# Depthwise-convolution products moved to ScalarE, branch projections reordered, attention block interleaved and finished by token rows

## The chip, the cores and the metric

The kernel runs on one core of a Trainium2 chip. The metric is the device time of one execution in microseconds (us). All weights and inputs come from HBM, and everything is float32.

## The reference, cut to what matters

Two transformer-like blocks follow each other on a 512 x 1024 activation. Each sublayer ends in a residual and a norm. The parts that the change touches are the middle sublayer of the first block and the last sublayer of the second:

```
u = modulate(x, sh2, sc2)
xr, gr, conf_in, gate_a, gate_b = split(u @ w_in)
xr = causal_depthwise_conv(xr, rnn_conv_w, rnn_conv_b)      # 4 taps
hr = rg_lru(xr, ...)                                        # gates r, i, then a scan over time
ya = (hr * gelu(gr)) @ rnn_w_proj
glu = conf_in[..., :D] * sigmoid(conf_in[..., D:])
hb = causal_depthwise_conv(glu, conf_dw_w, conf_dw_b)       # 31 taps
yb = silu(layer_norm(hb)) @ conf_w_proj
merged = sigmoid(gate_a) * ya + sigmoid(gate_b) * yb
x = layer_norm(alpha * x + (1 + g2) * (merged @ mix_w_out))
...
x = x + concat(ret, ssm) @ w_out
q = rms_norm(x, norm2_g) @ wq                               # 4 heads of 256
p = softmax(q k^T / 16);  o = p v                           # memory of 256 rows
x = x + o @ wo
return rms_norm(x, norm_f_g)
```

## The kernel before

Activations lie feature-major: eight tiles `[128 features, 512 tokens]` each. Every product `u @ W` is done in fp32r with both operands split into a high and a low part, `hi*hi + lo*hi + hi*lo`. So a chunk of 256 output features is 2 tiles x 8 k-tiles x 3 = 48 matmuls of 128x512. A weight chunk is loaded by SP into one of two raw slots, split high by ScalarE (`hi_step`, L559) and low by VectorE (`lo_step`, L978). `hi_step(ph, i, m, j)` prepares the chunk that stands two behind the one of that name, because it waits until TensorE has finished with the slot (`mm`). The order on each engine is written out by hand; engines meet at semaphores only. A PSUM bank pair is handed back through `free0`/`free1`.

The middle sublayer. TensorE's order is conf (8 chunks), xr (4), gr (4), the 16 r/i gate matmuls, gb (4), ga (4), the mean matmul `ln_shift(1)` (L1851), ya (4), the norm's statistics, yb (4), mix (4). The 31-tap convolution is done tile by tile beside them:

- GpSimd has tiles 0 to 2 (`POOL_CONV = 3`). Each tap is a `tensor_scalar` product into `conv_tap` (L464) and a `tensor_tensor` sum into `conv_out` (L466), each waiting for the one before it.
- VectorE has tiles 3 to 7. Each tap is one `scalar_tensor_tensor` whose accumulator is a PSUM bank (L1244), placed in batches (`conv_taps(n)`) between its other steps. Others of its steps are the 4-tap convolution (L1270, L1273: both tensor operands in SBUF), the products of the gated scan (L1302 to L1307) and the weight splits.
- GpSimd then sums the tiles for the mean (L430), which TensorE waits for before its first ya chunk.
- The sigmoid gates of gb and ga go to DRAM (`gate`, L721) and wait there for `bt_step` 16, because their staging tile lies over `rnn_i`. They come back as `sig_gate_a` and `sig_gate_b`.

The attention sublayer. After the eight residual tiles of wout_s, the root of the mean square is computed, then the eight tiles are scaled and split (L1407, L811, L1417), and only then does wq start. After wq the four heads run one behind the other: scores (L2143), row maximum (L1722), exponentials (L950), scaling (L1731), transposes (L2159), a copy (L955), values (L2166), a copy to `xa_out` (L1737) and its split. Then wo (4 chunks), the last norm's sums (L1877), the root, eight scaled tiles (L1749, L965), 32 transposes (L2177), and four stores of 512 KB.

Of the kernel before, what the change touches and what calls it, by code (L numbers as in the profile page):

```python
# [26 lines left out]
P = 128  # L27
D = 1024
KT = D // P
L = 512  # L30
# [8 lines left out]
POOL_CONV = 3  # L39
# [20 lines left out]
PHASES = [("ffn1", 22, 11), ("down1", 16, 4), ("conf", 8, 4), ("xr", 4, 2), ("gr", 4, 2),  # L60
          ("gb", 4, 2), ("ga", 4, 2), ("ya", 4, 2), ("yb", 4, 2), ("mix", 4, 2),
# [35 lines left out]
def build_program(nc, I, out):  # L97
    ctx = ExitStack()
    with ctx:
        BASE = 16512  # L100

        def at(name, kb, shape, dt=F32):
# [20 lines left out]
        TAP = at("conv_tap", H0 + 85, [P, L])  # L123
# [5 lines left out]
        STG = at("stage4k", H0 + 81, [P, 2, L])  # L129
# [9 lines left out]
        G = at("gelu_gate", T0, [P, KT, L])  # L139
        SGA = at("sig_gate_a", T0, [P, KT, L])  # L140
        SGB = at("sig_gate_b", T0, [P, KT, L])
# [98 lines left out]
        PS = ctx.enter_context(nc.psum_tensor("ps", [P, 8, 512], F32))  # L240
        MODP = PS[:, 4, 0:ADA_ALL]
# [18 lines left out]
                 "yb_sum mg_hi mg_lo lam_step conv31 conv31p s5_load s5_pow_load s5_expand s5_t "  # L260
# [5 lines left out]
                 "s_sum p_scaled p_t pt_ready o_mm oa_ready oh ol yo_ready out_t or_ready out_store "  # L266
# [15 lines left out]
        def _(sp):  # L282
# [82 lines left out]
            simple("gr", I["w_in"], D)  # L365
            simple("gb", I["w_in"], 5 * D)
            simple("ga", I["w_in"], 4 * D)
            simple("ya", I["rnn_w_proj"])
# [20 lines left out]
            for t in range(TT):  # L389
                sp.wait_ge(s["or_ready"], t + 1)  # L390
                sp.dma_start(out[0, t * P:(t + 1) * P, :], OR[:, t]).then_inc(s["out_store"], 16)
            sp.wait_ge(s["out_store"], 16 * TT)
# [3 lines left out]
        def _(pool):  # L396
# [55 lines left out]
            for f in range(POOL_CONV):  # L452
                pool.wait_ge(s["free1"], UB["conf"] + f // 2 + 1)
                if f == 0:
                    pool.wait_ge(s["pads_ready"], 1)
                for k in range(CONV_C):
                    src = GLU[:, f, k + 2:k + 2 + L]
                    w = col("conf_dw_w_a", 8 * k + f)
                    n = (2 * CONV_C - 1) * f + 2 * k
                    if k == 0:  # L460
                        nc.gpsimd.tensor_scalar(HB[:, f], src, w, col("conf_dw_b", f), ALU.mult, ALU.add).then_inc(s["conv31p"], 1)
                        continue
                    pool.wait_ge(s["conv31p"], n - 1)
# [5 lines left out]
            ln_sum(1, HB, lambda f: (s["conv31p"], (2 * CONV_C - 1) * (f + 1)) if f < POOL_CONV else  # L469
                   (s["conv31"], CONV_C * (f + 1 - POOL_CONV)))  # L470
# [74 lines left out]
            pool.dma_start(SGS[:], sgs_dram).then_inc(s["sgs_load"], 16)  # L545
            pool.wait_ge(s["mm"], CB["wq"])
            pool.dma_start(KA[:], ka_dram).then_inc(s["kv_load"], 16)
# [4 lines left out]
        def _(act):  # L552
# [21 lines left out]
            def ln_root(c):  # L574

                A(EPSC[:, 4 + c:5 + c], EPSC[:, 1:2], ACT.Sqrt)
                act.wait_ge(s["m_done"], c + 1)
                xsum = ln_tiles(c)[0]
                A(xsum[:], PS[:, 5], ACT.Square).then_inc(s["msq"], 1)
                act.wait_ge(s["var_ready"], c + 1)  # L580
                A(RT[:], xsum[:], ACT.Sqrt, bias=EPSC[:, 0:1]).then_inc(s["root_ready"], 1)
# [98 lines left out]
            with act.Fori(0, 4) as i:  # L680
# [6 lines left out]
            act.wait_ge(s["pads_ready"], 2)  # L687
            with act.Fori(0, 2) as i:
                for j in range(2):
                    hi_step("xr", i, 2, j)  # L690
                    act.wait_ge(s["mm"], CB["xr"] + 2 * i + j + 1)
                    A(XR[:, bass.ds(4 * i + 2 * j, 2), 8:8 + L], PS[:, 2 * j:2 * j + 2], ACT.Copy).then_inc(free[j], 1)
            with act.Fori(0, 2) as i:
                for j in range(2):
                    hi_step("gr", i, 2, j)
                    act.wait_ge(s["mm"], CB["gr"] + 2 * i + j + 1)
                    A(G[:, bass.ds(4 * i + 2 * j, 2)], PS[:, 2 * j:2 * j + 2], ACT.Gelu_apprx_tanh).then_inc(free[j], 1)

            for f in range(KT):
# [25 lines left out]
            gate("gb", sgb_dram, 0, 1)
# [15 lines left out]
            hi_step("ya", 0, 2, 1)
            hi_step("ya", 1, 2, 0)
            ln_squares(1, HB, 0, 7)
            hi_step("ya", 1, 2, 1)
            ln_squares(1, HB, 7, 8)
            ln_root(1)
            for f in range(KT + 1):
                if f < KT:
                    act.wait_ge(s["xn_ready"], 8 + f + 1)
                    A(HB[:, f], HB[:, f], ACT.Silu, scale=col("conf_ln_g", f), bias=col("conf_ln_b", f)).then_inc(s["conf_silu"], 1)  # L750
                if f:
                    act.wait_ge(s["conf_silu"], f)
# [187 lines left out]
            split_only("wout_s", 2, 2)  # L940
            norm(5, lambda f: pair_tile("wout_s", f), X, 1)

            rms_hi(4, 40, "norm2_g_2")
            plain("wq", QA)
            for h in range(XH):
                act.wait_ge(s["smax_ready"], 2 * h + 2)
                if h:
                    act.wait_ge(s["p_t"], h)
                for t in range(TT):
                    A(PB[:, t], PS[:, 4 + t // 2, (t % 2) * MEM:(t % 2 + 1) * MEM], ACT.Exp, scale=1.0 / 16, bias=XS[:, 1, t:t + 1],  # L950
                      accum_out=XS[:, 2 + h % 2, t:t + 1]).then_inc(s["exp_done"], 1)
                act.wait_ge(s["p_t"], h + 1)
# [3 lines left out]
                act.wait_ge(s["oa_ready"], h + 1)  # L956
                A(UH[:, 2 * h:2 * h + 2], OA[:], ACT.Copy).then_inc(s["oh"], 1)
            for i in range(2):
                for j in range(2):
                    if i == 0:  # L960
                        hi_step("wo", 0, 2, j)
            norm(6, lambda f: pair_tile("wo", f), X, 1)
            for f in range(KT):
                act.wait_ge(s["xn_ready"], 48 + f + 1)
# [1249 lines left out]
```

## Time and profile before

| | us |
|---|---|
| median of three runs (2372.64 to 2377.97) | 2374.69 |
| the profiled execution | 2371.09 |
| its span in the trace | 2369.1 |
| PE busy | 1953.8 (82%) |
| DVE busy | 1205.8 (51%) |
| ACT busy | 743.1 (31%) |
| POOL busy | 488.9 (21%) |

The span is what lies between the first and the last instruction; 2.0 us lie around it. PE is TensorE, DVE VectorE, ACT ScalarE, POOL GpSimd. Where two engines overlap, only the one that others wait for sets the time, so idle time is read by stage: the middle sublayer lies at 465 to 1036 us, the attention sublayer at 2153 us to the end.

### The profile page before, as it was taken

How to read it: one execution, taken by the hardware profiler on the slowest of the kernel's cores; microseconds unless marked ns; L12 is line 12 of the kernel's file. 1: busy time of each engine (PE TensorE's matmuls, PEld its weight loads, DVE VectorE, ACT ScalarE, POOL GpSimd, SP SyncE). 2: the span in 40 equal slices, each digit the busy share in tenths (PEclk: the TensorE clock that was granted, in tenths of full speed). 3: DMA queues.
4: the chain of work that ended last, by engine and by line, in shares of the span. 5: the costliest groups of instructions: out<-in, count | busy, mean ns of one | idle time of the engine just before them, and what ended most of it. 6: DMA issues, size and time to landing. Idle time of an engine off the chain costs nothing.

```text
span 2369.1 us, 23466 instructions
## 1 busy us (share of the span) xinstructions
PE 1953.8 (82%) x8848; PEld 1566.9 (66%) x8848; DVE 1205.8 (51%) x1463; ACT 743.1 (31%) x723; POOL 488.9 (21%) x386
## 2 busy tenths in 40 slices
PE   3999999799978085979999998869996677496877
PEld 2788878588757064758888877768873357474645
DVE  4555555639958476463323346633286764144223
ACT  2433322442453013244333335412341211122323
POOL 0311111279999910010000020010000030100000
PEclk8999999899989597989999999979997785698989
DMA  7455554223313211213333234452321070422200
GB/s 254 154 183 178 175 160 148 84 89 107 107 54 124 71 53 67 90 39 107 95 100 97 87 104 134 145 107 81 107 87 64 9 118 29 107 89 89 71 1 36
DMA packets 201885, 236.71 MB, mean 100 GB/s; under 512 B 5627, under 2 KB 184603, under 8 KB 200923
## 3 DMA queue, kind: packets, MB, share of 16 engines
q1 hardware_dynamic: 185067, 171.27, 22.9%
q0 software_dynamic: 14736, 54.04, 8.7%
q10 hardware_dynamic: 2016, 10.49, 1.2%
q8 instruction: 44, 0.72, 0.1%
q14 instruction: 22, 0.18, 0.0%
HBM read 220.58 MB, written 15.20 MB: 100 GB/s over the span
## 4 chain that ended last, share of the span: by engine, by line
PE 36%; DVE 8%; issue 4%; ACT 4%; DMA 4%; POOL 1%; DVEq 0%; ACTq 0%; SPq 0%; POOLq 0%
PE ps L1769 12%; PE ps L1937 9%; PE ps L1821 4%; PE ps L1787 2%; DMA w_raw<-in_s_glu_w 1%; PE ps L2121 1%; PE ps L2127 1%; DVE ret_root L1629 1%; ACT w_hi L559 1%; PE ps L2143 1%; PE ps L1877 1%; PE ps L2045 1%; DMA s_in<-u_scratch 1%; PE ps L2166 1%; DVE w_lo L978 1%
## 5 line engine op out<-in xcount | busy, mean ns | idle before, releaser
L978 DVE TENSOR_TENSOR w_lo<-w_raw,w_hi 128x2048 fp32r<-128x2048 f32 x160 | 375.3, 2345 | 774.3 <-ACT w_hi L559 757.5
L559 ACT ACTIVATE w_hi<-w_raw 128x2048 fp32r<-128x2048 f32 x158 | 302.4, 1914 | 977.5 <-PE ps L1769 547.6
L1769 PE MATMUL ps<-u_hi,w_hi 128*128 128x512 f32 x960 | 383.7, 400 | 72.7 <-DVE u_lo L1692 31.3
L1769 PE MATMUL ps<-u_lo,w_hi 128*128 128x512 f32 x960 | 378.5, 394 | 0.0
L1769 PE MATMUL ps<-u_hi,w_lo 128*128 128x512 f32 x960 | 378.2, 394 | 0.0
L1769 PEld LDWEIGHTS ps<-u_hi,w_hi 128*128 128x128 f32 x960 | 184.0, 192 | 117.8 <-issue 54.8
L1937 PE MATMUL ps<-u_hi,w_hi 128*128 128x512 f32 x656 | 256.9, 392 | 0.3 <-ACT silu_gate L637 0.3
L1937 PE MATMUL ps<-u_lo,w_hi 128*128 128x512 f32 x656 | 255.8, 390 | 0.0
L1937 PE MATMUL ps<-u_hi,w_lo 128*128 128x512 f32 x656 | 255.8, 390 | 0.0
L1769 PEld LDWEIGHTS ps<-u_lo,w_hi 128*128 128x128 f32 x960 | 183.7, 191 | 39.1 <-issue 1.3
L1769 PEld LDWEIGHTS ps<-u_hi,w_lo 128*128 128x128 f32 x960 | 183.1, 191 | 39.0
L464 POOL TENSOR_SCALAR conv_tap<-glu,param_cols 128x512 f32<-128x512 f32 x90 | 187.6, 2085 | 8.8
L1821 PE MATMUL ps<-hid_hi,w_hi 128*128 128x512 f32 x352 | 140.6, 400 | 0.6 <-DVE hid_lo L1148 0.6
L1937 PEld LDWEIGHTS ps<-u_hi,w_hi 128*128 128x128 f32 x656 | 123.5, 188 | 26.0 <-ACT silu_gate L637 0.7
L1937 PEld LDWEIGHTS ps<-u_hi,w_lo 128*128 128x128 f32 x656 | 123.6, 188 | 25.8
L1937 PEld LDWEIGHTS ps<-u_lo,w_hi 128*128 128x128 f32 x656 | 123.6, 188 | 25.4
L1821 PE MATMUL ps<-hid_hi,w_lo 128*128 128x512 f32 x352 | 137.7, 391 | 0.0
L1821 PE MATMUL ps<-hid_lo,w_hi 128*128 128x512 f32 x352 | 137.6, 391 | 0.0
L466 POOL TENSOR_TENSOR conv_out<-conv_out,conv_tap 128x512 f32<-128x512 f32 x90 | 126.9, 1409 | 7.5
L1244 DVE SCALAR_TENSOR_TENSOR ps<-glu,param_cols,ps 128x512 f32<-128x512 f32 x145 | 109.5, 755 | 4.7
L408 POOL DMA_DIRECT2D ada_raw<-in_ada_w x56 | 40.1, 717 | 347.2 <-DVE ada_acc L1082 295.7
L1082 DVE SCALAR_TENSOR_TENSOR ada_acc<-ada_raw,silu_c,ada_acc 128x512 f32<-128x512 f32 x98 | 74.2, 757 | 8.1 <-DMA ada_raw<-in_ada_w 5.5
(423 smaller groups left out, 2800.2 us busy)
## 6 DMA issues: line engine op xcount, KB each, us to landing
w_raw<-in_w_in SPq DMA_DIRECT2D x44, 1024.0 KB, 5.2
ada_raw<-in_ada_w POOLq DMA_DIRECT2D x56, 512.0 KB, 5.0
w_raw<-in_ffn_w_gate SPq DMA_DIRECT2D x22, 1024.0 KB, 5.3
w_raw<-in_ffn_w_up SPq DMA_DIRECT2D x22, 1024.0 KB, 5.3
w_raw<-in_ffn_w_down SPq DMA_DIRECT2D x32, 704.0 KB, 4.6
ada_first<-in_ada_w SPq DMA_DIRECT2D x8, 1024.0 KB, 11.3
w_raw<-in_w_out SPq DMA_DIRECT2D x8, 1024.0 KB, 5.0
w_raw<-in_rnn_w_proj SPq DMA_DIRECT2D x4, 1024.0 KB, 5.6
```

The source lines that it names most:

```text
L408: pool.dma_start(ADRAW[:, q % 2], wk8(I["ada_w"])[:, 2 * q:2 * q + 2, bass.ds(2 * D + 512 * i, 512)]).then_inc(ada_load[q % 2], 16)
L464: nc.gpsimd.tensor_scalar(TAP[:], src, w, None, ALU.mult).then_inc(s["conv31p"], 1)
L466: nc.gpsimd.tensor_tensor(HB[:, f], HB[:, f], TAP[:], ALU.add).then_inc(s["conv31p"], 1)
L559: A(WHI[:, slot], WRAW[:, slot], ACT.Copy).then_inc(s["w_hi"], 1)
L978: V.tensor_tensor(WLO[:, slot], WRAW[:, slot], WHI[:, slot].bitcast(F32), ALU.subtract).then_inc(s["w_lo"], 1)
L1082: ins = V.scalar_tensor_tensor(out=acc, in0=ADRAW[:, q % 2, kk], scalar=SC[:, k:k + 1], in1=acc, op0=ALU.mult, op1=ALU.add)
L1244: ins = V.scalar_tensor_tensor(out=dst, in0=src, scalar=w, in1=HACC, op0=ALU.mult, op1=ALU.add)
L1629: V.reciprocal(RRT[:], RRT[:]).then_inc(s["rn"], 1)
L1769: ins = M(PS[:, 2 * j + t, 0:n], w[:, j, at_:at_ + P], a[:, k, 0:n], start=(q == 0), stop=(q == 3 * KT - 1))
L1787: ins = M(PS[:, 2 * j + t], w[:, j, at_:at_ + P], a[:, k], start=(k == 0 and q == 0), stop=(k == KT - 1 and q == 2))
L1821: ins = M(PS[:, 2 * (j // 2)], w[:, j % 2, P * kk:P * kk + P], a[:, k], start=(k == 0 and q == 0), stop=(k == FT - 1 and q == 2))
L1937: ins = M(PS[:, 2 * j + t], w[:, j, at_:at_ + P], a[:, k], start=(q == 0), stop=(q == 3 * KT - 1))
```

## The change

- The convolution's tiles are dealt differently: 0, 2, 4, 6 to GpSimd, 1, 3, 5, 7 to VectorE. The products of GpSimd's tiles are made by ScalarE (`conv_products`) into a ring of four tap tiles; GpSimd only adds (120 sums of 128x512; the first tap goes straight to `conv_out`).
- The phases run conf, xr, gb, ri, ga, gr, ya, yb. The gate's staging tile has a place of its own, and the gelu of gr is applied pairwise at the end. ScalarE's loops are written out. The mean and statistics matmuls stand between ya chunks.
- In attention, wq runs on x unscaled by the root; the root is multiplied in when q is read out of PSUM. The heads are interleaved with the wq chunks; wo is computed with tokens on the partitions, against x transposed earlier, and each 128-token row block is normalised and stored by halves.

```diff
-POOL_CONV = 3
+POOL_CONV = (0, 2, 4, 6)
+DVE_CONV = (1, 3, 5, 7)
@@ gpsimd
-            for f in range(POOL_CONV):
...
-                    nc.gpsimd.tensor_scalar(TAP[:], src, w, None, ALU.mult).then_inc(s["conv31p"], 1)
-                    pool.wait_ge(s["conv31p"], n)
-                    nc.gpsimd.tensor_tensor(HB[:, f], HB[:, f], TAP[:], ALU.add).then_inc(s["conv31p"], 1)
+            for i, f in enumerate(POOL_CONV):
+                for k in range(1, CONV_C):
+                    m = (CONV_C - 1) * i + k - 1
+                    pool.wait_ge(s["conv_tap"], CONV_C * i + k + 1)
+                    if m:
+                        pool.wait_ge(s["conv31p"], m)
+                    nc.gpsimd.tensor_tensor(HB[:, f], HB[:, f], TAP[:, m % 4], ALU.add).then_inc(s["conv31p"], 1)
@@ scalar
+            def conv_products(n):
+                for f, k in products[made[0]:made[0] + n]:
...
+                        if m >= 4:
+                            act.wait_ge(s["conv31p"], m - 3)
+                        ins = A(TAP[:, m % 4], src, ACT.Copy, scale=w)
+                    ins.then_inc(s["conv_tap"], 1)
+            for i in range(4):
+                hi_step("conf", i, 2, 0)
...
+                if i:
+                    conv_products(6)
+                hi_step("conf", i, 2, 1)
+                if i:
+                    conv_products(6)
+            for n in range(4):
+                hi_step("xr", n // 2, 2, n % 2)
...
+                conv_products(6)
+            for n in range(4):
+                gate("gb", sgb_dram, n)
+                conv_products(6)
...
+            gate("ga", sga_dram, 0)
...
+            for n in range(1, 4):
+                gate("ga", sga_dram, n)
+                conv_products(6)
+            for n in range(4):
...
+                A(G[:], PS[:, 2 * (n % 2):2 * (n % 2) + 2], ACT.Gelu_apprx_tanh).then_inc(free[n % 2], 1)
+                hi_step("gr", n // 2, 2, n % 2)
+                conv_products(6)
+                act.wait_ge(s["yf_ready"], n + 1)
+                A(YH[:, 2 * n:2 * n + 2], XC[:, 2 * n:2 * n + 2], ACT.Copy).then_inc(s["yh_ready"], 2)
@@ vector
-                if i >= 2:
-                    conv_taps((16, 15)[i - 2])
+                if i:
+                    conv_taps(18)
...
+            lo_step("ga", 0, 2, 0)
+            for f in range(4):
+                scan(f)
+            lo_step("ga", 0, 2, 1)
+            for f in range(4, KT):
+                scan(f)
+            for j in range(2):
+                lo_step("ga", 1, 2, j)
+                conv_taps(6)
+            for n in range(4):
...
+                V.tensor_tensor(xp, xp, G[:], ALU.mult).then_inc(s["yf_ready"], 1)
+                lo_step("gr", n // 2, 2, n % 2)
+                conv_taps(3)
...
+            conv_taps(14)
+            lo_step("ya", 0, 2, 0)
+            ya_pair(0)
+            lo_step("ya", 0, 2, 1)
+            ya_pair(1)
...
+            ln_shift(1, HB, 0, 8)
+            lo_step("ya", 1, 2, 0)
+            ya_pair(2)
+            def after_tile(f):
+                conf_lo(f)
+                if f == 3:
+                    ya_pair(3)
+                    lo_step("ya", 1, 2, 1)
@@ tensor
+            gemm_chunk("ya", 0, 0, YH, YL, ready=lambda k: (s["yl_ready"], k + 1))
+            gemm_chunk("ya", 0, 1, YH, YL)
             ln_shift(1)
+            gemm_chunk("ya", 1, 0, YH, YL)
             ln_stats(1, HB, 7)
+            gemm_chunk("ya", 1, 1, YH, YL)
+            gemm_after("yb", 2, CHI, CLO, lambda k: (s["yl_ready"], 8 + k + 1))
...
-            norm(5)
-            pe.wait_ge(s["ul_ready"], 40)
-            gemm("wq", 2, UH, UL)
+            gemm_chunk("wq", 0, 0, UH, UL, ready=lambda k: (s["ul_ready"], 32 + k + 1))
+            pe.wait_ge(s["sq_used"], 8 * 5 + 6)
...
+            gemm_chunk("wq", 0, 1, UH, UL)
...
+            xa_scores(0)
+            gemm_chunk("wq", 1, 0, UH, UL)
+            xa_scores(1)
+            probs(0)
+            gemm_chunk("wq", 1, 1, UH, UL)
+            xa_scores(2)
+            values(0)
+            probs(1)
+            xa_scores(3)
+            values(1)
+            probs(2)
+            x_tokens(0)
+            values(2)
+            x_tokens(1)
+            probs(3)
+            x_tokens(2)
+            values(3)
+            x_tokens(3)
+            out_rows(0, range(6))
+            out_rows(1, range(6))
+            out_rows(0, (6, 7))
+            out_rows(1, (6, 7))
+            out_rows(2, range(KT))
+            out_rows(3, range(KT))
@@ the body of out_rows
+                        for q, (a, w) in enumerate(((UH, wh), (UL, wh), (UH, wl))):
+                            ins = M(PS[:, ROW_BANK[t] + half].rearrange("p (c n) -> p c n", c=2), a[:, k, t * P:(t + 1) * P],
+                                    w[:, :, 256 * k:256 * k + 256], start=(k == 0 and q == 0), stop=(k == KT - 1 and q == 2))
@@ vector, the end of one row block
+                V.tensor_tensor(xr, xr, PS[:, ROW_BANK[t] + half], ALU.add).then_inc(s["row_sum"], 1)
...
+                    V.scalar_tensor_tensor(out=xr, in0=xr, scalar=XS[:, 12, t:t + 1], in1=GROW[:, half * L:half * L + L],
+                                           op0=ALU.mult, op1=ALU.mult).then_inc(s["or_ready"], 1)
```

## Rows read from the trace of the kernel before

**Rows 1.** Stretches: start:end, us, busy us (instructions) of PE, PEld, DVE, ACT, POOL, granted clock, DMA.
```profile
487.00:640.00 153.00, 152.84 (x673) 126.38 (x674) 115.89 (x104) 49.44 (x35) 144.40 (x81) 1.00 0.34 109
640.00:695.00 55.00, 38.73 (x129) 24.17 (x128) 35.66 (x36) 29.52 (x39) 52.10 (x32) 0.86 0.13 41
764.50:829.40 64.90, 0.04 (x1) 0.04 (x1) 34.79 (x40) 7.10 (x10) 61.24 (x39) 0.53 0.21 73
829.40:942.00 112.60, 80.19 (x298) 60.73 (x298) 73.32 (x90) 28.84 (x34) 9.72 (x6) 0.83 0.16 56
2225.00:2290.00 65.00, 39.95 (x126) 26.66 (x125) 20.83 (x23) 18.77 (x42) 0.00 (x0) 0.82 0.05 16
```

**Rows 2.** Waits of TensorE: its line, whom it waited for, us in total, times, longest.
```profile
PE ps L1851 <- POOL conf_x_sum L430: 64.9, 1, 64.9
PE ps L1769 <- DVE u_lo L1417: 16.2, 1, 16.2
PE ps L1769 <- ACT stage4k L721: 13.8, 1, 13.8
```

**Rows 3.** TensorE in order of time inside ya: start, duration, instruction, idle before.
```profile
853.46 0.39 PE L1769 MATMUL ps<-y_lo,w_hi 128*128 128x512 f32 x1
853.68 0.39 PE L1769 MATMUL ps<-y_hi,w_lo 128*128 128x512 f32 x1
858.18 0.79 PE L1769 MATMUL ps<-y_hi,w_hi 128*128 128x512 f32 x1 [4.11 <-DVE ya L1327]
858.78 0.63 PE L1769 MATMUL ps<-y_lo,w_hi 128*128 128x512 f32 x1
```

**Rows 4.** One source line's instructions: count, ns min/median/max, first and last start.
```profile
L466 POOL TENSOR_TENSOR conv_out<-conv_out,conv_tap x90: 1261/1295/3132, 492.8 to 821.2; 128x512 f32<-128x512 f32 x90
L1244 DVE SCALAR_TENSOR_TENSOR ps<-glu,param_cols,ps x145: 741/756/757, 536.4 to 897.1; 128x512 f32<-128x512 f32 x145
```

**Rows 5.** Groups by line from 571 to 614 us, DVE then POOL.
```profile
L1273 DVE SCALAR_TENSOR_TENSOR xr_conv<-xr_pad,param_cols,xr_conv x24 | 27.9, 1228 | 0.0
L978 DVE TENSOR_TENSOR w_lo<-w_raw,w_hi 128x2048 fp32r<-128x2048 f32 x4 | 11.5, 2868 | 0.0
L466 POOL TENSOR_TENSOR conv_out<-conv_out,conv_tap 128x512 f32<-128x512 f32 x10 | 13.7, 1374 | 0.8
```

**Rows 6.** ScalarE in order of time: the norm's square, a plain copy, the last wout_s split.
```profile
905.42 0.60 ACT L579 ACTIVATE conf_x_sum<-ps 128x512 f32<-128x512 f32 x1 [2.91 <-PE ps L1869]
915.18 0.61 ACT L753 ACTIVATE y_hi<-conv_out 128x512 fp32r<-128x512 f32 x1
2153.16 1.91 ACT L559 ACTIVATE w_hi<-w_raw 128x2048 fp32r<-128x2048 f32 x1 [8.96 <-PE ps L1769]
```

**Rows 7.** VectorE in order of time: scan steps, fourth normalised tile, a split, last residual.
```profile
739.33 0.68 DVE L1302 TENSOR_TENSOR rnn_t<-rnn_t,xr_conv 128x512 f32<-128x512 f32 x1
740.05 1.51 DVE L1305 TENSOR_TENSOR_SCAN xr_conv<-rnn_a,rnn_t 128x512 f32<-128x512 f32 x1
923.91 0.69 DVE L1337 TENSOR_TENSOR y_lo<-conv_out,y_hi 128x512 fp32r<-128x512 f32 x1 [1.41 <-ACT y_hi L753]
2309.86 2.29 DVE L978 TENSOR_TENSOR w_lo<-w_raw,w_hi 128x2048 fp32r<-128x2048 f32 x1 [11.29 <-ACT w_hi L559]
2340.50 1.22 DVE L1656 TENSOR_TENSOR x_res<-x_res,ps 128x1024 f32<-128x1024 f32 x1 [9.66 <-PE ps L1769]
```

**Rows 8.** TensorE in order of time in the first head: scores, transposes, values.
```profile
2237.59 3.72 PE L2143 MATMUL ps<-xa_k,xa_q 128*128 128x256 f32 x16 [3.49 <-ACT xa_probs L950]
2241.15 1.04 PE L2159 MATMUL ps<-ident,xa_probs 128*128 128x128 f32 x8
2243.30 3.70 PE L2166 MATMUL ps<-xa_probs_t,xa_v 128*128 128x512 f32 x8 [1.11 <-ACT xa_probs_t L955]
```

**Rows 9.** DMA issues: engine, count, KB each, us from issue to landing.
```profile
sig_gate_a<-sga_scratch ACTq DMA_DIRECT2D x1, 2048.0 KB, 8.1
out<-out_rows SPq DMA_DIRECT2D x4, 512.0 KB, 2.9
```

More of the change, by code:

```diff
@@ L389, in _ @@
             for t in range(TT):
-                sp.wait_ge(s["or_ready"], t + 1)
-                sp.dma_start(out[0, t * P:(t + 1) * P, :], OR[:, t]).then_inc(s["out_store"], 16)
-            sp.wait_ge(s["out_store"], 16 * TT)
+                for half in range(2):
+                    sp.wait_ge(s["or_ready"], 2 * t + half + 1)
+                    cols = slice(half * L, half * L + L)
+                    sp.dma_start(out[0, t * P:(t + 1) * P, cols], XROW[:, t, cols]).then_inc(s["out_store"], 16)
+            sp.wait_ge(s["out_store"], 32 * TT)
         @block.gpsimd
@@ L678, in _ @@
             ln_modulate_hi(0, 0, 8, 0)
-            with act.Fori(0, 4) as i:
+            products = [(f, k) for f in POOL_CONV for k in range(CONV_C)]
+            made = [0]
+            def conv_products(n):
+                for f, k in products[made[0]:made[0] + n]:
+                    src = GLU[:, f, k + 2:k + 2 + L]
+                    w = col("conf_dw_w_a", 8 * k + f)
+                    i = POOL_CONV.index(f)
+                    if k == 0:
+                        act.wait_ge(s["free1"], UB["conf"] + f // 2 + 1)
+                        ins = A(HB[:, f], src, ACT.Identity, scale=w, bias=col("conf_dw_b", f))
+                    else:
+                        m = (CONV_C - 1) * i + k - 1
+                        if m >= 4:
+                            act.wait_ge(s["conv31p"], m - 3)
+                        ins = A(TAP[:, m % 4], src, ACT.Copy, scale=w)
+                    ins.then_inc(s["conv_tap"], 1)
+                    made[0] += 1
+            act.wait_ge(s["pads_ready"], 2)
+            for i in range(4):
                 hi_step("conf", i, 2, 0)
@@ L955, in _ @@
                 A(PT[:], PS[:, 6:8], ACT.Copy).then_inc(s["pt_ready"], 1)
[L956 to L964, printed above, removed]
-                A(YO[:, f], UT[:, f % 2], ACT.Identity, scale=col("norm_f_g_2", f)).then_inc(s["yo_ready"], 1)
@@ new lines, in x_row @@
+            def x_row(t):
+                act.wait_ge(s["mm"], CB["wo"] + t + 1)
+                A(XROW[:, t], PS[:, 2:4].rearrange("p b n -> p (b n)"), ACT.Copy).then_inc(s["xrow_ready"], 1)
+            exps(0)
+            hi_step("wq", 1, 2, 0)
+            probs_t(0)
+            exps(1)
+            hi_step("wq", 1, 2, 1)
+            wo_hi(0)
+            exps(2)
+            out_hi(0)
+            probs_t(1)
+            exps(3)
+            out_hi(1)
+            probs_t(2)
+            x_row(0)
@@ new lines, in _ @@
+            wo_hi(1)
+            out_hi(2)
+            x_row(1)
+            probs_t(3)
+            x_row(2)
+            out_hi(3)
+            x_row(3)
+            A(XS[:, 13, 0:1], EPSC[:, 1:2], ACT.Sqrt)
+            for t in range(TT):
+                for half in range(2):
+                    act.wait_ge(s["row_sum"], 2 * t + half + 1)
+                    if t:
+                        act.wait_ge(s["row_ss"], 3 * t - 2 + 2 * half)
+                    A(SQ[:, half], XROW[:, t, half * L:half * L + L], ACT.Square, accum_out=XS[:, 8 + half, t:t + 1]).then_inc(s["row_ss"], 1)
+                    if half == 0:
+                        act.wait_ge(s["row_ss"], 3 * t + 1)
+                        A(XS[:, 10, t:t + 1], XS[:, 8, t:t + 1], ACT.Identity, scale=1.0 / D, bias=EPSC[:, 1:2]).then_inc(s["row_ss"], 1)
+                act.wait_ge(s["row_ss"], 3 * t + 3)
+                A(XS[:, 11, t:t + 1], XS[:, 9, t:t + 1], ACT.Sqrt, scale=1.0 / D, bias=XS[:, 10, t:t + 1]).then_inc(s["root_ready"], 1)
@@ L1024, in ln_normalize @@
                 dve.wait_ge(s["root_ready"], c + 1)
-                dve.wait_ge(s["ln_step"], ln_step(V.reciprocal(RSTD[:], RT[:])))
+                root, rstd = ln_roots(c)
+                dve.wait_ge(s["ln_step"], ln_step(V.reciprocal(rstd[:], root[:])))
                 def scaled(f):
@@ L1227, in _ @@
             ln_normalize(0, X, ln_modulate_lo(0, 0, 8))
-            taps = [(f, k) for f in range(POOL_CONV, KT) for k in range(CONV_C)]
+            taps = [(f, k) for f in DVE_CONV for k in range(CONV_C)]
             done = [0]
@@ L1274, in _ @@
                             ins.then_inc(s["conv4"], 1)
[L1275 to L1278 removed]
+            for n in range(4):
+                lo_step("gb", n // 2, 2, n % 2)
+                conv_taps(8)
             for f in range(KT):
@@ new lines, in _ @@
+            query(0)
+            query(1)
+            lo_step("wq", 0, 2, 1)
+            row_max(0)
+            scale_probs(0)
+            query(2)
+            lo_step("wq", 1, 2, 0)
+            row_max(1)
+            scale_probs(1)
+            query(3)
+            row_max(2)
+            lo_step("wq", 1, 2, 1)
+            out_lo(0)
+            scale_probs(2)
+            wo_lo(0)
+            row_max(3)
+            out_lo(1)
+            scale_probs(3)
+            out_lo(2)
+            wo_lo(1)
```

332 lines of the change are left out of this document (165 added, 167 removed).

## Prediction

> **What bounds the kernel now.** I read the stretches first, then TensorE's waits, then each engine in order of time inside the two stages that change. While TensorE is fed it sets the pace: from 487 to 640 us it is busy 152.84 of 153 us with 673 matmuls at the full 2.4 GHz, 0.227 us each [rows 1], so a chunk of 48 costs 10.9 us. Two stretches are not like that. After ga it stands still for 64.9 us, in which GpSimd is busy 61 us and VectorE only 35 [rows 1]: the mean waits for GpSimd's convolution tiles [rows 2]. Up to the end of yb's first two chunks at 942 us it is busy 80 of 112.6 us more [rows 1]. In the heads (2225 to 2290) no engine is busy over 62% [rows 1]: a serial chain. So TensorE's queue is the frame of the sum, and each stall in it is a term.
>
> **Middle sublayer, without contention.** GpSimd's 90 sums, each behind its product, ran from 492.8 to 821.2 us [rows 4]. Now it makes 120 sums and no products, typically 1.30 us, 1.5 with handoffs and the long ones [rows 4]: 180 us. ScalarE's product has no row; a plain copy of this shape takes 0.61 [rows 6]. I take 0.65 (0.6 to 0.9, with a scale), so a batch of six takes ScalarE about 4.3 us, held by the ring of four for its last two. That fits into 10.9 us beside a split and an evacuation. Batches start at about 499 us and come one per chunk, the last with gr's last chunk; the sums end soon after, at about 757, plus 7 us for the five mean sums. The mean is wanted only after two ya chunks, at 779. The 64.9 us go, and GpSimd is not late next.
>
> The walk on TensorE: 640 plus 1 us for VectorE's tighter conf (three batches of 18 taps at 0.76 [rows 4] instead of 16 and 15). The r/i matmuls take 20 us, one more than before, since ScalarE starts them behind a batch. Eight chunks of ga and gr, 87 us. The 13.8 us wait [rows 2] goes with the staging tile's own place; what is late next is the split behind the `bt` products, 1.5 us, and 0.4 twice behind the scans. So gr ends at 750, where ga ended at 764.5 before. Then:
> - the first ya chunk does 18 matmuls (4.1 us) and waits for the last y_lo pair, which comes 9.1 us after gr (gelu 1.1, product 1.2, w_hi then w_lo 3.0, three taps 2.4, y_lo 1.3): 5.0 of stall. After a stall of 4.1 us TensorE ran matmuls of 0.63 instead of 0.39 us [rows 3]; twelve such cost 2.5. The two chunks end at 779;
> - VectorE waits for `sig_gate_a` before its last 14 taps: issued at 757, 8.1 us [rows 9], then taps to 776, split, product: the third chunk runs 780.4 to 791.3. The eight shifts end at 789.5, the squares' sums (seven of 1.4) at 795, the statistics at 800.5, and the fourth ya chunk runs beside the normalisation, to 811.4;
> - yb's first pair needs both weight slots. The second is split only behind the fourth tile. That tile came 19.2 us after the square of the mean [rows 6, 7], now at 818.8; w_hi 1.9, the ya product 1.2 and w_lo 2.3 on top give 824.3. The pair, 96 matmuls and a slow start, ends at 849.
>
> Before it ended at 942 [rows 1]: 93 us less.
>
> **What the sums cost VectorE.** The trace shows that a GpSimd sum holds up VectorE when that reads two tensors from SBUF: the 4-tap steps L1273 take 1.228 us, the weight split 2.868 [rows 5], where taps with the accumulator in PSUM never exceed 0.757 [rows 4] and a split with GpSimd idle takes 2.29 [rows 7]. From 571 to 614 that is 24 x 0.47 + 4 x 0.58 = 13.6 us over ten sums: 1.36 us each, a sum's own length [rows 5]. An xr chunk takes about 7.7 us of VectorE by itself (eight steps of about 0.7, a split of 2.3), and 11.1 with two and a half sums. With six it takes 15.9, against TensorE's 10.9: VectorE becomes the bound of xr. Following its queue, the splits come 2, 7, 3 and 5 us late, in all 17; I take 15 (0 if the sums fall into VectorE's gaps, 19 if none does). In ga, two batches of six sums meet the scans (0.68 and 1.51 per tile [rows 7]) and two splits: at most 12 x 1.3 = 16 us. Whether the scan instruction is held is not visible; I take 10 (0 to 16). In gr and ya a few sums meet the product, the split and y_lo: 3 (0 to 5). Restarts at the lower clock after these stalls are mostly absorbed by the next wait: 3 (0 to 8). Together 31 (0 to 48); the saving here is 62.
>
> The page "SBUF — State Buffer" of the Trainium skill (section "SBUF: two separate sides") states this as an exclusive lock: a VectorE instruction with two SBUF inputs and a GpSimd one that reads SBUF shut each other out for their whole length. By that rule every coincidence costs in full, also in the scans, and the 31 would be 48. The rows agree for L1273 and the split; for the scan they leave it open. The rule speaks against this change, as it turns GpSimd from half products (which let L1273 pass) into nothing but sums, so its outcome is a rival below.
>
> **Attention.** Gone: the norm before wq (26 us from wout_s's end at 2153.2 [rows 6] to wq, of which 16.2 is its last wait [rows 2]), the idle time of the heads, and the final norm. The walk, with scores 3.7, transposes 1.0, values 3.7 [rows 8] and x transposes 1.1:
> - first wq chunk 2153.2 to 2164.6, 0.5 late for the last tiles; three norm matmuls 2.6; second chunk to 2178.1. The root and its reciprocal are ready at 2172; q's pairs are 1.2 each. KA, VA and the gain row are DMAs beside the first chunks. Scores 0, third chunk, scores 1, transposes, fourth chunk: 2208.5;
> - scores 2, values 0, transposes 1, scores 3, values 1, transposes 2 and x 0: 2226.6. There ScalarE's queue (exponentials, o high, copy) is 1.1 late for values 2. The rest of the heads ends at 2239.6;
> - wo is 192 matmuls of 512 columns as before: 43.5, to 2283. That its moving operand comes in two pieces has no row; I take nothing (0 to 10);
> - the tail: sum 0.7, square with its read-out 1.0, root 0.3, reciprocal 0.25, two products 1.5, the last 256 KB store 3.2 against 2.9 for 512 KB with its wait [rows 9]. End 2290.4.
>
> Before, TensorE finished wo at 2340.5 [rows 7] and the span ended at 2369.1. That saves 78.7 (65 to 80, as any late handoff in the heads adds its own length).
>
> **Sum.** 2371.1 - 62 - 78.7 = 2230.4 for an execution like the profiled one. That lay 3.6 under the median of its runs, so 2374.7 - 140.7 = 2234.
>
> **Rivals.**
> 1. *No contention to speak of*: the ring lets sums fall into VectorE's gaps. For it: in conf VectorE mostly does PSUM taps. Against it: xr has no gaps. 2374.7 - 93 - 78.7 = 2203.
> 2. *Full lock*, the rule above: 2374.7 - (93 - 48) - 70 = 2260, with the long side of attention too. For it: 1.3 to 1.4 per sum. Against it: sums after VectorE's late steps run beside taps.
> 3. *The heads stay serial*: an order on one engine meets another's (ScalarE's out_hi and w_hi before exponentials), so that attention gives back half, and the middle stage has the full lock: 2374.7 - 45 - 40 = 2290. Against it: my walk finds one wait of 1.1.
> 4. *Slower*: GpSimd still bounds the mean, as each sum waits for a product that stands in ScalarE's queue behind a weight split and an evacuation, and ScalarE in turn waits for the ring. If the sums come at pitch p, yb's pair ends at 502 + 120p + 7 for the mean + 68 to the end. That exceeds 942 + 79 from p = 3.7. At p = 3.9 the time is 2399. For it: single sums reached 3.1 us [rows 4]. Against it: the median is 1.3, and only every sixth product stands behind a split.
>
> **Chances.** Forecast (2215 to 2250) 0.5; rival 1 0.24; rival 2 0.18; rival 3 0.05; rival 4 0.02; 0.01 for no change. A difference under 0.2% (5 us) can't be told from none here. Faster 0.97, same 0.01, slower 0.02. The range reaches from just under rival 1 to a little over rival 2: 2200 to 2268.
>
> **What would show it.** TensorE's 64.9 us wait at L1851 gone, and no wait on `conf_x_sum` over 3 us in this sublayer. In xr, waits of TensorE on `w_lo` of 10 to 19 us in all, L1273 at 1.7 to 2.0 us; two more of 4 to 5 us in ga. GpSimd's sums end before ya's first chunk does. A gap of 10 to 13 us ahead of yb on `w_lo`. From wout_s's end to the end of the span 137 us, with TensorE idle under 6 us before the tail. The forecast is wrong if L1273 stays near 1.2 us (then rival 1), if a wait on `conf_x_sum` remains (rival 4's way), or if the heads show waits over 2 us each (rival 3).

## The result, and the profile after

The changed kernel takes 2217.86 us (median of 4 runs, 2211.68 to 2220.46) against 2374.03: a ratio of 0.9336, 95% interval 0.9313 to 0.9359, or 156 us less. Forecast: 2234, range 2200 to 2268. The profiled execution took 2219.47 us with a span of 2217.5, 151.6 under the span before.

The page of the changed kernel, busy time by engine, first; then the granted clock in 40 slices:

```profile
PE 1928.9 (87%) x8822; PEld 1556.5 (70%) x8822; DVE 1186.4 (53%) x1423; ACT 800.4 (36%) x838; POOL 376.8 (17%) x329
PEclk8999999989999988989999999998999679559999
```

GpSimd has 30 more convolution sums and no products and is busy less; ScalarE has taken the products. TensorE was busy for 1928.9 us of the span; the other 288.6 us are its idle time. These are all its waits from 500 to 900 us, the stretch in which [rows 2] had 64.9 and 13.8:

```profile
PE ps L1894 <- DVE w_lo L1053: 16.4, 6, 7.2
PE ps L1912 <- DVE w_lo L1053: 12.8, 1, 12.8
PE ps L1894 <- DVE y_lo L1393: 8.1, 2, 7.4
PE ps L2092 <- ACT rnn_a L739: 5.7, 1, 5.7
PE ps L1989 <- POOL conf_squares_sum L451: 4.9, 1, 4.9
PE ps L1894 <- DVE rnn_i L1432: 1.5, 1, 1.5
```

The wait on `conf_x_sum` is gone and none on it took its place. What stands there now is VectorE: w_lo, the second half of the weight split, is late in seven places. The stretches of the changed kernel (columns as in [rows 1]): the middle sublayer in two parts, then wq with the heads, and wo with the tail.

```profile
500.00:650.00 150.00, 140.74 (x603) 114.65 (x602) 137.57 (x123) 82.25 (x101) 113.88 (x72) 0.98 0.33 105
650.00:850.00 200.00, 164.07 (x632) 122.80 (x631) 147.02 (x138) 112.84 (x139) 99.42 (x60) 0.92 0.26 89
2084.00:2168.00 84.00, 81.74 (x362) 62.59 (x361) 40.88 (x34) 37.19 (x59) 1.62 (x3) 1.00 0.28 94
2168.00:2217.50 49.50, 43.62 (x193) 35.77 (x191) 12.86 (x21) 10.69 (x28) 0.00 (x0) 0.96 0.11 43
```

In the first, VectorE is busy for 137.57 of 150 us, close to being the bound; in the third, TensorE is busy for 81.74 of 84, where the heads in [rows 1], which stood apart from wq, had 39.95 of 65. Two ends carry the comparison: yb's first pair (its first two chunks) ends at 877.46 us (942 before), and wout_s at 2084.6 (2153.2 before). So the middle sublayer brings 64.6 us (forecast 62), the attention block 83.0 (forecast 78.7), and 4.0 lie between, in stages the change does not touch.

The groups of VectorE and GpSimd from 480 to 900 us (count | busy us, mean ns | idle before):

```profile
L1053 DVE TENSOR_TENSOR w_lo<-w_raw,w_hi 128x2048 fp32r<-128x2048 f32 x31 | 82.9, 2673 | 49.9 <-ACT w_hi L562 49.9
L1349 DVE SCALAR_TENSOR_TENSOR xr_conv<-xr_pad,param_cols,xr_conv x24 | 34.9, 1519 | 0.0
L1374 DVE TENSOR_TENSOR_SCAN xr_conv<-rnn_a,rnn_t 128x512 f32<-128x512 f32 x8 | 13.7, 1709 | 0.3
L1346 DVE TENSOR_SCALAR xr_conv<-xr_pad,param_cols x8 | 8.8, 1142 | 0.0
```

```profile
L467 POOL TENSOR_TENSOR conv_out<-conv_out,conv_tap 128x512 f32<-128x512 f32 x120 | 199.2, 1660 | 143.4 <-ACT conv_tap L699 128.1
```

L1346 is the first of the four taps, L1349 the other three. The latter (L1273 before) went from 1.228 [rows 5] to 1.519 us, and GpSimd's sum from 1.409, its mean over the same stretch before, to 1.660, as if each held up the other; the experiments test it. GpSimd waits 128.1 us for products. It is not the bound.

### The profile page after: what moved, and what is told of

Same layout as the page of the kernel before. It is cut to its first block, busy times and chain, and to the rows that moved or that the text cites. A ratio compares the mean times of both kernels' runs of the same rounds, so it can differ in the third digit from the quotient of the medians.

```text
span 2217.5 us, 23475 instructions
## 1 busy us (share of the span) xinstructions
PE 1928.9 (87%) x8822; PEld 1556.5 (70%) x8822; DVE 1186.4 (53%) x1423; ACT 800.4 (36%) x838; POOL 376.8 (17%) x329
## 4 chain that ended last, share of the span: by engine, by line
PE 38%; DVE 7%; issue 4%; DMA 4%; ACT 3%; POOL 1%; DVEq 1%; ACTq 0%; SPq 0%; POOLq 0%
PE ps L1894 11%; PE ps L2062 10%; PE ps L1946 4%; PE ps L2311 2%; PE ps L1912 2%; DMA w_raw<-in_s_glu_w 1%; PE ps L2249 1%; PE ps L2255 1%; ACT w_hi L562 1%; DVE ret_root L1713 1%; PE ps L2173 1%; DMA s_in<-u_scratch 1%; PE ps L2205 1%; DVE s_state L1676 1%; DVE w_lo L1053 1%
## 5 line engine op out<-in xcount | busy, mean ns | idle before, releaser
L1894 PE MATMUL ps<-u_hi,w_hi 128*128 128x512 f32 x896 | 358.8, 400 | 56.4 <-DVE u_lo L1776 30.8
L1894 PE MATMUL ps<-u_lo,w_hi 128*128 128x512 f32 x896 | 353.2, 394 | 0.0
L1894 PE MATMUL ps<-u_hi,w_lo 128*128 128x512 f32 x896 | 352.9, 394 | 0.0
L2062 PE MATMUL ps<-u_hi,w_hi 128*128 128x512 f32 x656 | 256.2, 391 | 0.3 <-ACT silu_gate L640 0.3
L2062 PE MATMUL ps<-u_hi,w_lo 128*128 128x512 f32 x656 | 255.2, 389 | 0.0
L2062 PE MATMUL ps<-u_lo,w_hi 128*128 128x512 f32 x656 | 255.2, 389 | 0.0
L1894 PEld LDWEIGHTS ps<-u_hi,w_hi 128*128 128x128 f32 x896 | 171.4, 191 | 98.7 <-issue 49.0
L467 POOL TENSOR_TENSOR conv_out<-conv_out,conv_tap 128x512 f32<-128x512 f32 x120 | 199.2, 1660 | 143.4 <-ACT conv_tap L699 128.1
L1894 PEld LDWEIGHTS ps<-u_lo,w_hi 128*128 128x128 f32 x896 | 171.5, 191 | 36.2 <-issue 1.2
L1894 PEld LDWEIGHTS ps<-u_hi,w_lo 128*128 128x128 f32 x896 | 170.9, 191 | 36.4
L2062 PEld LDWEIGHTS ps<-u_hi,w_lo 128*128 128x128 f32 x656 | 123.2, 188 | 25.8
L2062 PEld LDWEIGHTS ps<-u_hi,w_hi 128*128 128x128 f32 x656 | 123.2, 188 | 25.6 <-ACT silu_gate L640 0.8
L2062 PEld LDWEIGHTS ps<-u_lo,w_hi 128*128 128x128 f32 x656 | 123.2, 188 | 25.3
L699 ACT ACTIVATE conv_tap<-glu,param_cols 128x512 f32<-128x512 f32 x120 | 79.6, 715 | 33.1 <-POOL conv_out L467 30.5
L1320 DVE SCALAR_TENSOR_TENSOR ps<-glu,param_cols,ps 128x512 f32<-128x512 f32 x116 | 87.6, 755 | 6.2 <-DMA sig_gate_a<-sga_scratch 2.5
```

What stands on the lines that cost most here:

```text
L467: nc.gpsimd.tensor_tensor(HB[:, f], HB[:, f], TAP[:, m % 4], ALU.add).then_inc(s["conv31p"], 1)
L699: ins = A(TAP[:, m % 4], src, ACT.Copy, scale=w)
L1320: ins = V.scalar_tensor_tensor(out=dst, in0=src, scalar=w, in1=HACC, op0=ALU.mult, op1=ALU.add)
L1894: ins = M(PS[:, 2 * j + t, 0:n], w[:, j, at_:at_ + P], a[:, k, 0:n], start=(q == 0), stop=(q == 3 * KT - 1))
L2062: ins = M(PS[:, 2 * j + t], w[:, j, at_:at_ + P], a[:, k], start=(q == 0), stop=(q == 3 * KT - 1))
```

## The experiments

The changed kernel itself was run beside two of the three sets as their base. Times are medians of four runs.

**The base.** 

> The changed kernel once more, on the chip of the other runs of this set, as their base. Every theory: 2218, within 5.

2217.43 us, ratio 0.9359 (0.9332 to 0.9386). Here yb's first pair ended at 872.93, 4.5 us before that of the profiled execution above; the difference is there when the r/i matmuls start (648.2 against 653.0), and xr's waits account for most of it: the same kernel varies there by a few us from one execution to another. The second base, beside the two last kernels below:

> The changed kernel once more, as the base of the two runs beside it. Every theory: 2218, within 6.

2220.92 us, ratio 0.9359 (0.9343 to 0.9374).

**Is it the lock?**

```
- tensor_tensor(HB[:, f], HB[:, f], TAP[:, m % 4], ALU.add)
+ tensor_tensor(HB[:, f, 0:16], HB[:, f, 0:16], TAP[:, m % 4, 0:16], ALU.add)
```

> GpSimd's 120 convolution sums add 16 columns of 512 and leave the other 496 out; every wait and every other operation stays. Theory A (GpSimd's sums and VectorE's operations with two SBUF inputs hold each other up, and this makes w_lo late in xr and ga): the 4-tap operations of VectorE come at a pitch of 1.2 us or less instead of 1.54, the scans go back from 2.2 to about 1.25, the 7.2 wait in ga and the 10 of waits in xr and gb go, and the whole is 2195, from 2186 to 2204. Theory B (VectorE is late since ScalarE makes its batches of products before the next weight split): the batches stay, the waits stay, and the time is 2214 to 2219.

2194.07 us, ratio 0.9248 (0.9231 to 0.9266), as theory A had it. VectorE's groups in that kernel, same stretch:

```profile
L1053 DVE TENSOR_TENSOR w_lo<-w_raw,w_hi 128x2048 fp32r<-128x2048 f32 x33 | 75.5, 2289 | 81.8 <-ACT w_hi L562 81.8
L1349 DVE SCALAR_TENSOR_TENSOR xr_conv<-xr_pad,param_cols,xr_conv x24 | 16.2, 748 | 0.0
L1374 DVE TENSOR_TENSOR_SCAN xr_conv<-rnn_a,rnn_t 128x512 f32<-128x512 f32 x8 | 9.8, 1224 | 0.3
L1346 DVE TENSOR_SCALAR xr_conv<-xr_pad,param_cols x8 | 4.0, 542 | 0.0
```

Every operation with two SBUF inputs is back at one length: 748 ns instead of 1519, 1224 instead of 1709, 2289 instead of 2673. So is the first tap, which reads one tensor from SBUF and writes to SBUF: 542 instead of 1142. The waits for w_lo at L1894 are gone; the 12.8 at L1912 stays, and so does the wait for `rnn_a`, at 5.2. yb's first pair ends at 847.94. ScalarE's batches were all still there. Its waits for the ring became shorter too, so this run alone does not exclude that ScalarE was what came late. For xr the next run does. For ga the trace of the changed kernel does: w_hi was ready at 712.2 us, and VectorE came to its w_lo at 723.9, behind four scans that ran beside sums.

**Which operations are held?**

```
+ acc = PS[:, 4 + t]
+ dst = XC[:, f] if k == CONV_R - 1 else acc
- scalar_tensor_tensor(out=dst, in0=src, scalar=w, in1=dst, ...)
+ scalar_tensor_tensor(out=dst, in0=src, scalar=w, in1=acc, ...)
```

> VectorE's 4-tap convolution keeps its running sum in two free PSUM banks, and only the fourth tap writes xr_conv. Theory A (the lock is taken only by an operation with two SBUF inputs): the operations fall from 1.54 to about 0.76 each, 6 us go from each chunk of xr, the w_lo waits of xr (3.5, 1.7, 1.1 and 2.3) go, and the time is 2210, from 2206 to 2213. Theory B (ScalarE's batches make the splits late): VectorE then waits for w_hi instead, and the time is 2215 to 2219.

2208.28 us, ratio 0.9301 (0.9271 to 0.9331), beside 2217.43 and 0.9359 (0.9332 to 0.9386) for the base: 9 us less, and the intervals only just part. With one of the two inputs in PSUM the step takes half the time, although GpSimd's sums run beside it in full:

```profile
L1349 DVE SCALAR_TENSOR_TENSOR ps<-xr_pad,param_cols,ps 128x512 f32<-128x512 f32 x16 | 10.9, 743 | 0.0
L1347 DVE TENSOR_SCALAR ps<-xr_pad,param_cols 128x512 f32<-128x512 f32 x8 | 6.1, 801 | 0.0
```

The first tap, which now writes to PSUM, takes 801 ns: less than the 1142 beside sums, more than the 542 that it takes into SBUF beside short ones. So theory A had the held operations too narrow: the first tap has one SBUF input and was held as well.

All waits for w_lo in xr are gone; the 7.2 in ga and one of 0.6 stay. yb's pair ends at 862.59, 10.3 us before that of the base. It leaves nothing out, so it is a better kernel too.

**What ScalarE's products bring.**

```
- A(TAP[:, m % 4], src, ACT.Copy, scale=w)                       # ScalarE
+ nc.gpsimd.tensor_scalar(TAP[:, 0], src, w, None, ALU.mult)     # GpSimd, before each sum
```

> GpSimd makes the products of its four tiles by itself again, ScalarE makes none; the order of the projections stays. By the rival's formula of the prediction (yb's first pair ends at 577 + 120p) and the pitch of product and sum in the kernel before, 3.7 us, the pair ends at 1021 and the time is 2361; if product and sum ran at their shortest, 2.9, it ends at 925 and the time is 2265. Expected near the upper end, 2345. If ScalarE's products are not what brought the gain, but the order of the projections, it stays under 2235.

2341.38 us, ratio 0.9867 (0.9848 to 0.9886). GpSimd's groups:

```profile
L473 POOL TENSOR_SCALAR conv_tap<-glu,param_cols 128x512 f32<-128x512 f32 x120 | 240.5, 2004 | 11.8
L475 POOL TENSOR_TENSOR conv_out<-conv_out,conv_tap 128x512 f32<-128x512 f32 x120 | 166.9, 1391 | 10.0
```

The pitch is (240.5 + 166.9 + 11.8 + 10.0) / 120 = 3.58 us; the slower rival's formula then gives 577 + 120 x 3.58 = 1006 for the end of yb's first pair, and the trace shows 998.55 (this profile is of the slowest of the four executions, 2350.25 us). So the formula is sound where GpSimd is the bound. The rival's own way to such a pitch, sums that wait for products in ScalarE's queue, was not what this run made; in the changed kernel the 120 sums take from 502.3 to 788.4 us, a pitch of 2.38. With the products back on GpSimd, the new order and GpSimd's fourth tile end this pair 57 us after that of the kernel before: four tiles need ScalarE's products.

How much of the 64.6 us the new order would bring without them, with three tiles on GpSimd as before, was not run. It need not be little. In the kernel before the sums ended at 822.5 us; 7 us for the mean and the prediction's 68 behind it give an end at 897.5 instead of 942, an estimate, and only if VectorE has its five tiles ready by then (its last tap ended at 898.6, but it stood idle for 45.05 us while TensorE waited for the mean).

**The two parts apart.** The kernel before with the one part or the other, whole.

> The kernel before with the attention part of the change alone; the middle sublayer is as before. If the two parts are independent, as the prediction sums them, the attention part brings the 83.0 us that the two traces differ by from wout_s's end on: 2373 less 83 is 2290, from 2285 to 2295. If the parts share something (the clock, the stage buffers, a queue), it comes out by more than 6 us elsewhere.

> The kernel before with the middle sublayer's part alone (products on ScalarE, sums on GpSimd, the other order of the branch projections); the attention block is as before. Independent parts: yb's first pair ends 64.6 us sooner, so 2308, or 2304 if the 4 us that the traces differ by between there and wout_s's end belong to it too. A part that the attention change shares with it would show as more than 6 us off 2306.

Attention alone: 2292.00, ratio 0.963 (0.9607 to 0.9652). The middle sublayer alone: 2303.69, ratio 0.969 (0.967 to 0.9711). The savings add up to 3.7% + 3.1% = 6.8%, against 6.4 to 6.6% for both at once in the three comparisons, so they are independent within some 0.4%. The traces say it more closely. From wout's restart behind `glu_lo` to the end of the span pass 258.5 us in the kernel before (2110.64 to 2369.1), 174.3 with the attention part alone (2118.09 to 2292.4) and 174.2 with both (2043.26 to 2217.5). With the middle part alone, yb's pair ends at 872.85, with both at 872.93 in the second profile.

**The wait ahead of yb.**

```
- scaled(0);  for f: scaled(f + 1); each(f)
+ scaled(0); scaled(1);  for f: scaled(f + 2); each(f)     # conv branch's normalisation only
```

> The changed kernel with one change: in the conv branch's normalisation VectorE scales two tiles ahead of the split instead of one. Theory A (the 12.8 us wait for w_lo ahead of yb is the ping-pong of VectorE and ScalarE at 2.7 to 3.4 us per tile, behind which the split of the fourth ya chunk's successor stands): a tile then costs 1.5 to 2.1 us, yb's first pair starts some 8 us sooner, and the time is 2209, from 2205 to 2212. Theory B (the wait is the end of the fourth ya chunk plus the split itself, 1.9 on ScalarE and 2.3 on VectorE, and a table of queues behind it): nothing moves by more than 2, 2215 to 2219.

2215.71 us; no base ran on that chip, and the ratio of 0.9315 (0.9297 to 0.9334) overlaps that of the changed kernel. In its trace the wait fell from 12.8 to 9.3 us:

```profile
PE ps L1914 <- DVE w_lo L1053: 9.3, 1, 9.3
```

Neither theory has the size. The tiles did go faster, but w_hi cannot start before ya's fourth chunk leaves its slot. It ended at 840.4, VectorE came to the w_lo at 844.6, behind two tiles and ya's product, and ended it at 846.8. The pair ended at 871.98, 1.0 us before that of the base's profile.

**Five edits together.** Beside the two above: `lo_step("ga", 1, 2, 0)` between the sixth and seventh scan; `conv_products(1)` behind each of the eight i gates in place of the batch behind gb's last gate; y_hi and y_lo of gr's last pair ahead of the split and the taps.

> Five edits of the changed kernel together: the 4-tap sum in PSUM (9 us by its own run), two tiles ahead (8 expected), the weight split of ga's third chunk put between the sixth and seventh scan of the recurrence on VectorE (it is ready 12 us before VectorE comes to it, and PE waits 7.2 for it), the batch of products after gb's last gate spread over the r and i gates one by one (4 of the 5.7 us wait for rnn_a), and for gr's last pair the y_hi and y_lo halves put ahead of the weight split, products and taps (4 of 8.1). The theory that each wait stands alone on the chain adds them: 2217 less 9, 8, 7, 4 and 4 is 2185. The rival, that GpSimd's sums (idle only 128 us in all) become the bound of ya's mean as gr comes sooner, gives back the 7, the 4 and the 4: 2200.

2192.78, ratio 0.9234 (0.9202 to 0.9266). Once more, with the base beside it:

> The five edits once more, now with the changed kernel beside them on one chip. The traces say that yb's first pair ends 24 to 29 us sooner than in the changed kernel: 2191, from 2188 to 2195.

2195.70, ratio 0.925 (0.9235 to 0.9266), against 2220.92 and 0.9359 (0.9343 to 0.9374) of the base: 25 us less. yb's pair ends at 848.16, against 872.90. Its largest waits from 500 to 900 us:

```profile
PE ps L1927 <- DVE w_lo L1059: 10.2, 1, 10.2
PE ps L1909 <- DVE u_lo L1452: 5.1, 1, 5.1
PE ps L1909 <- DVE w_lo L1059: 4.9, 3, 4.0
PE ps L1909 <- DVE y_lo L1405: 3.6, 2, 3.0
PE ps L2104 <- ACT rnn_i L743: 2.9, 1, 2.9
```

The 7.2 in ga became 4.0, y_lo's 8.1 became 3.6, and `rnn_a`'s 7.2 turned into 2.9 and 1.5 on the r and i gates. (u_lo's 5.1 lies behind yb and only came into this window.) The median is 0.7 us above the range that was expected for it. The sum of the expected single effects was 32, of which 8 stood for the two tiles, where 3.5 had come by their own run; 25 came. GpSimd's sums ended at 768 and did not bound the mean, so the expected rival was not it: each wait left a rest.

**Seven edits.** On top: `lo_step("ga", 1, 2, 1)` ahead of ga's last taps; ya's last product and split behind the second tile on VectorE, its w_hi ahead of the fourth on ScalarE.

> The five edits and two more. VectorE splits ga's fourth chunk ahead of its twelve taps (PE waits 4.0 us for it in the kernel of five edits), and in the normalisation the evacuation of ya's fourth chunk and the split behind it come after the second tile on VectorE and ahead of the fourth on ScalarE. The theory that VectorE's order alone makes both waits: the 4.0 goes, the 9.1 ahead of yb falls to some 4 (a split of 1.9 and one of 2.3 behind the end of ya's chunk), and the time is 2182, from 2178 to 2186. The rival, that the sums on GpSimd and the chain of gr's halves come next and take what ga gives: only the 5 of yb are left, 2187.

2198.14, ratio 0.9262 (0.9247 to 0.9278): no gain over five edits, and neither theory's time. In ga the longest wait for w_lo only went from 4.0 to 3.1. The wait ahead of yb did fall to 6.8 and yb's pair ended at 842.98, 5.2 sooner. Of this lead 2.5 us were left at the end of qk, and retention lost more than that. TensorE in order of time there, first with five edits, then with seven; behind the same wait of 16.65 us:

```profile
1705.62 4.63 PE L2220 MATMUL ps<-qk_rot 64*128 64x512 f32 x8 [16.65 <-DVE ret_scores L1722]
1710.18 4.03 PE L2242 MATMUL ps<-ret_scores,v_rows 128*128 128x512 f32 x8
...
1715.96 2.42 PE L2220 MATMUL ps<-qk_rot 64*128 64x512 f32 x8
```

```profile
1703.15 4.63 PE L2219 MATMUL ps<-qk_rot 64*128 64x512 f32 x8 [16.65 <-DVE ret_scores L1721]
1707.70 4.63 PE L2241 MATMUL ps<-ret_scores,v_rows 128*128 128x512 f32 x8
...
1715.03 4.63 PE L2219 MATMUL ps<-qk_rot 64*128 64x512 f32 x8
1719.59 4.38 PE L2241 MATMUL ps<-ret_scores,v_rows 128*128 128x512 f32 x8
```

Eight matmuls take 4.63 us after the wait and 2.42 once the clock is back from 1.2 to 2.4 GHz. In the one execution it was back some 9 us after the wait, in the other after some 20. The granted clock from 1705 to 1730 us, five edits, then seven:

```profile
1705.00:1730.00 25.00, 20.94 (x54) 0.83 0.11 32
```

```profile
1705.00:1730.00 25.00, 24.31 (x51) 0.63 0.09 29
```

Retention took 106.5 us in the first and 111.7 in the second. That makes a loss of 2.7 us out of the lead of 2.5, most of the 3.7 us between the two profiled executions; whether it is what kept the medians together, the runs do not show, since each has one profile.

## Why the prediction was right, step by step

- *Products off GpSimd, the mean no longer late.* Right. The sums ended at 788, not 757: they ran at 1.66 us, not 1.5, and waited for products. This miss of 31 us cost nothing, as the order had left room for it. The mean is wanted at 805.8 and did not wait. The product took 0.715 us, not 0.65.
- *The walk without contention, pair ends at 849.* The kernel of short sums, which is that case, ended it at 847.94.
- *Contention 31 us.* 877.46 less 847.94 is 29.5 (25.0 by the second profile). Behind the kernel of short sums the changed one is 13.0 us when r/i start, 14.6 when ga starts and 28.9 at the mean matmul. So 13.0 fell in xr and gb (forecast 15) and 14.3 in ga, gr and ya (forecast 13, and 3 for restarts anywhere). From conf to gb the waits for w_lo were 9.7 us in six, and gb ended at 653.2, 13.3 later than the same three branches before. In ga there was one wait of 7.2 where two of 4 to 5 were expected, and y_lo's wait was 7.45 + 0.62 (forecast 5).
- *1.36 us per sum.* Mis-sized. VectorE's four xr chunks took 54.3 us beside 27 sums (571.7 to 626.0) and take 4 x 7.09 = 28.4 beside short ones: 0.96 each. A 4-tap step beside a sum takes 1.78 us instead of 0.74, 1.04 more. The 1.36 of [rows 5] was the price of a product and a sum together: in the kernel before, the same step took 1.18 us beside a product alone, so products did not let L1273 pass, though the prediction says so. L1349's mean is 1.52, where 1.7 to 2.0 was the sign named, since some of the steps still ran between sums.
- *The scan.* It was left open (10, from 0 to 16) and is now shown: it is held. The trace before had the sign already: its scans took 1.22 to 1.60 us, and the 1.51 of [rows 7], taken as the scan's own length, was a held one. In the changed kernel the first four ran while GpSimd was idle or only just starting, the last four beside sums:

```profile
702.21 1.22 DVE L1374 TENSOR_TENSOR_SCAN xr_conv<-rnn_a,rnn_t 128x512 f32<-128x512 f32 x1
...
710.25 2.21 DVE L1374 TENSOR_TENSOR_SCAN xr_conv<-rnn_a,rnn_t 128x512 f32<-128x512 f32 x1
```

  The rule of the Trainium skill (page "SBUF — State Buffer", section "SBUF: two separate sides") holds here for every operation with two SBUF inputs that met sums: VectorE and GpSimd make each other wait, and one input in PSUM frees the operation (743 against 1519 ns). Its "whole length" is not what the trace shows, and the trace decides: where 4-tap steps and sums alternate, from 579.3 to 586.1 us, both come every 1.70 us, and 0.74 and 1.26 in turn would make 2.00. The full-lock rival was too high by this price and, it seems, by the count: ScalarE's ring feeds GpSimd in batches, GpSimd stood idle from 666 to 704 us, and so half of the scans and all products of `bt` met no sum.
- *r/i 20 us.* It took 23, mis-sized by a wait of 5.7. ScalarE makes a batch of six products before the first gates, in the changed kernel from 656.5 to 660.8, while PE's first gate stands ready:

```profile
656.47 3.17 ACT L699 ACTIVATE conv_tap<-glu,param_cols 128x512 f32<-128x512 f32 x5 [0.40 <-ACT stage4k L728]
660.06 0.72 ACT L699 ACTIVATE conv_tap<-glu,param_cols 128x512 f32<-128x512 f32 x1 [0.42 <-POOL conv_out L467]
660.69 0.67 ACT L739 ACTIVATE rnn_a<-ps,param_cols 128x512 f32<-128x512 f32 x1
```

- *The gap ahead of yb, 10 to 13 us.* 12.8. The forecast had its maker right, the second slot's split behind the fourth tile; two tiles ahead takes off only 3.5 of it.
- *Attention, 137 us from wout_s's end.* 132.9, right in its make. The heads took 58.9 (forecast 61.5) with two waits, 2.0 and 0.3; wo took 43.8 for 192 matmuls, so its moving operand in two pieces costs nothing that shows; the tail 5.9 (forecast 7.3, of which its listed terms make 6.95). The last row block in order of time, VectorE's part:

```profile
2211.66 0.69 DVE L1868 TENSOR_TENSOR x_by_token<-x_by_token,ps 128x512 f32<-128x512 f32 x1 [4.75 <-PE ps L2311]
2213.46 0.16 DVE L1870 RECIPROCAL xa_small<-xa_small 128x1 f32<-128x1 f32 x1 [1.11 <-ACT xa_small L1043]
2213.66 1.41 DVE L1873 SCALAR_TENSOR_TENSOR x_by_token<-x_by_token,xa_small,norm_f_row 128x512 f32<-128x512 f32 x2
```

- *The 16 us between forecast and median.* By the spans: 2.6 in the middle, 4.3 in attention, 4.0 in untouched stages. The other 5.2 is how the medians lie to the profiled executions: the kernel before ran 3.6 above its own, the changed one 1.6 below.

Left open: the 4.0 us in untouched stages. The kernel with the attention part alone comes to wout's restart behind `glu_lo` 7.5 us later than the kernel before, though nothing ahead of it was changed, and retention alone differs by 5 between two kernels that share its code, so one profile each can't tell it from chance. Left open too is how the middle sublayer's gain divides between the products' move and the new order.

## What to carry to other kernels

Before work is moved to GpSimd beside a busy VectorE, count VectorE's operations with two SBUF inputs in that stretch, and the GpSimd sums that will run beside them: in xr a sum cost VectorE 0.96 us, three quarters of its shortest length. A running sum kept in free PSUM banks freed the steps, at the price of the two banks and of a first tap of 0.80 us instead of 0.54. After such a move look for the late half of a weight split: where TensorE waits for it though the first half is long ready, one line's place in VectorE's order is worth 3 to 5 us here (7.2 to 4.0 in ga, 8.1 to 3.6 for y_lo). Gains under some 5 us can be lost in stages further on, so read them in the stretch itself and not in the total.

## What the runs showed of the hardware that was not expected

- TENSOR_TENSOR_SCAN is held by GpSimd like the other operations with two SBUF inputs: 1.22 us alone, 2.20 beside sums.
- The first tap, a TENSOR_SCALAR with one SBUF input and its output in SBUF, is held too: 0.53 us alone, 1.50 beside sums, and 0.80 beside sums with its output in PSUM.
- GpSimd pays as well: from 560 to 628 us its 128x512 sum had a mean of 1.71 us in the base's profile and 1.47 with xr's running sums in PSUM; its shortest is 1.26.
- A GpSimd product (one SBUF input) slows VectorE's 4-tap steps less than a sum does: in the kernel before, such a step took 1.18 us beside a product and 1.78 beside a sum, 0.74 beside neither.
- After a wait of 16.65 us on the same program text, the clock came back after about 9 us in one execution and 20 in another.
